# A block of paged key scores cut into two halves, with a prompt pair's scores between them

## What is computed

```python
def block(args):                       # prompt: 16 heads of 64, query blocks of 128
    qb, cb, pb = args
    logits = (jnp.einsum('bqhd,bkhd->bhqk', qb, k).astype(jnp.float32) * FOX_SCALE
              + cb[..., :, None] - cum[:, :, None, :])
    logits = jnp.where(pb[:, None] >= k_pos[None, :], logits, NEG_INF)
    p = jax.nn.softmax(logits, axis=-1).astype(v.dtype)
    return jnp.einsum('bhqk,bkhd->bqhd', p, v)
...
k_past = k_pool[page_table].reshape(b, -1, FOX_HEADS, FOX_DH)      # sample: 16 pages of 128 keys each
v_past = v_pool[page_table].reshape(b, -1, FOX_HEADS, FOX_DH)
logits = (jnp.einsum('bqhd,bkhd->bhqk', q.astype(k_all.dtype), k_all).astype(jnp.float32) * FOX_SCALE
          + suffix[:, :, None, :] - suffix[:, :, p_len:, None])
p = jax.nn.softmax(logits, axis=-1).astype(v_all.dtype)
o = jnp.einsum('bhqk,bkhd->bqhd', p, v_all).reshape(b, n, FOX_HEADS * FOX_DH).astype(x.dtype)
```

## Time and profile before

| | us |
|---|---|
| median of three runs | 3735.44 |
| lowest, highest | 3734.29, 3739.70 |
| the profiled execution | 3732.01 |
| its span in the trace | 3730.4 |
| steady part of the FoX stage in it | 1156 to 1567 |

### The profile page before, as it was taken

The page is one execution under the profiler, slowest core; times in us unless marked ns, Lnnn a source line. Parts: engine busy times, 40 slices in busy tenths (PEclk is TensorE's granted clock), DMA queues, the critical chain, the costliest instruction groups (busy, mean ns, idle before and its releaser), DMA issues.

```text
span 3730.4 us, 65316 instructions
## 1 busy us (share of the span) xinstructions
PE 3241.8 (87%) x27579; PEld 2943.6 (79%) x27579; DVE 1602.6 (43%) x2086; ACT 971.4 (26%) x1423; POOL 244.7 (7%) x331
## 2 busy tenths in 40 slices
PE   7998899997977888869999854479999899889997
PEld 6897799997864444469999743479998798779997
DVE  2324544324224444354442399664432422464422
ACT  2301322223202233232222244332222310232222
POOL 0000000003300000000000078000000000000000
PEclk9996899998987888889999887689999898789998
DMA  3213223322337776632323110123232120322321
GB/s 95 57 34 102 74 86 88 91 74 65 89 105 269 303 297 257 236 94 85 90 86 89 45 45 23 40 63 89 86 89 63 57 79 23 113 68 87 91 86 47
DMA packets 466048, 369.42 MB, mean 99 GB/s; under 512 B 16777, under 2 KB 429886, under 8 KB 465884
## 3 DMA queue, kind: packets, MB, share of 16 engines
q1 hardware_dynamic: 449808, 348.72, 29.6%
q10 hardware_dynamic: 11980, 17.28, 1.4%
q0 software_dynamic: 4096, 1.06, 0.3%
HBM read 348.68 MB, written 17.26 MB: 98 GB/s over the span
## 4 chain that ended last, share of the span: by engine, by line
PE 81%; DVE 9%; issue 5%; ACT 3%; DMA 1%; ACTq 0%; DVEq 0%; SPq 0%
PE acc L716 55%; PE acc L697 6%; PE acc L1049 3%; DVE big L1297 3%; PE acc L1092 2%; PE acc L912 2%; PE acc L900 1%; DVE rstd L1327 1%; PE acc L1010 1%; PE acc L776 1%; PE acc L1001 1%; PE acc L985 1%; DVE yT L1361 1%; PE acc L1225 1%; PE acc L990 1%
## 5 line engine op out<-in xcount | busy, mean ns | idle before, releaser
L716 PE MATMUL acc<-h_hi,wsp 128*128 128x272 f32 x5632 | 944.0, 290 | 66.1 <-DVE h_lo L1583 66.1
L1319 DVE TENSOR_TENSOR wsp<-ring,wsp 128x1024 fp32r<-128x1024 f32 (+1 forms) x320 | 416.8, 1305 | 1169.1 <-ACT wsp L1880 1169.1
L716 PEld LDWEIGHTS acc<-h_hi,wsp 128*128 128x128 f32 x5632 | 798.6, 190 | 68.7 <-issue 68.4
L1880 ACT ACTIVATE wsp<-ring 128x1024 fp32r<-128x1024 f32 (+1 forms) x320 | 358.6, 1124 | 1303.2 <-PE acc L716 1294.1
L716 PE MATMUL acc<-h_lo,wsp 128*128 128x272 f32 x3328 | 690.2, 289 | 0.0
L716 PEld LDWEIGHTS acc<-h_lo,wsp 128*128 128x128 f32 x3328 | 527.2, 190 | 0.0
L716 PE MATMUL acc<-g_hi,wsp 128*128 128x272 f32 x2816 | 473.9, 290 | 24.0 <-DVE g_lo L1578 24.0
L716 PEld LDWEIGHTS acc<-g_hi,wsp 128*128 128x128 f32 x2816 | 401.3, 191 | 24.9 <-issue 24.9
L716 PE MATMUL acc<-i_hi,wsp 128*128 128x272 f32 x1536 | 265.6, 295 | 37.2 <-DVE i_lo L1347 32.4
L716 PE MATMUL acc<-g_lo,wsp 128*128 128x272 f32 x1408 | 292.7, 290 | 0.0
L716 PEld LDWEIGHTS acc<-i_hi,wsp 128*128 128x128 f32 x1536 | 225.0, 196 | 39.7 <-issue 35.6
(11 more groups left out here) (288 smaller groups left out, 3104.6 us busy)
## 6 DMA issues: line engine op xcount, KB each, us to landing
ring<-in_ffn_w SPq DMA_DIRECT2D x176, 512.0 KB, 3.8
mix<-in_cache_fox_k SPq DMA_DIRECT2D x128, 512.0 KB, 6.9
ring<-in_cache_fox_v SPq DMA_DIRECT2D x106, 512.0 KB, 6.9
ring<-in_ffn_w SPq DMA_DIRECT2D x64, 704.0 KB, 4.7
ring<-in_conv_w SPq DMA_DIRECT2D x24, 512.0 KB, 3.9
mix<-in_cache_fox_v SPq DMA_DIRECT2D x22, 512.0 KB, 6.6
ring<-in_gla_wr SPq DMA_DIRECT2D x16, 512.0 KB, 4.0
ring<-in_gla_wv SPq DMA_DIRECT2D x16, 512.0 KB, 4.1
```

Of the source, the lines that this page charges most:

```text
L716: last = pe.matmul(acc[:, bank + h, 0:HALF], wsp[:, s, w, k * P:(k + 1) * P], rhs[:, k0 + k, h * HALF:(h + 1) * HALF], start=start and k = ...
L1319: dve.tensor_tensor(wsp[:, s, 1, 0:tiles * P], ring[:, slot, 0:tiles * P], wsp[:, s, 0, 0:tiles * P], ALU.subtract).then_inc(wlo_done, 1)
L1880: act.activation(wsp[:, slot % SPLITS, 0, 0:tiles * P], ring[:, slot, 0:tiles * P], ACT.Copy)\
```

## The change

sample_scores is cut in two functions. sample_bias has the bias matmuls and the waits; sample_scores(G, heads, new) has the key scores of two of the four head groups, and with new = True the new keys behind them. In an even step the order becomes: bias, first half, turn_output, scores_of_pair, second half with new keys, and only there ksc_full is set. The weighings stand one by one between the item transposes. The transpose of the new probabilities moves from turn() into weigh(v, 0).

On VectorE the pair's maxima come first in an even step, then the reciprocals, then the transposes and the maximum of z; in an odd step transpose 5 stands between the two maxima. On ScalarE the eviction of a block to z moves behind the pair's exponentials, and the exponential of z behind the copies of the pair's transposed probabilities. No instruction's form changes and none is added except a few waits.

```diff
-            def sample_scores(G):
+            def sample_bias(G):
...
                 pe.wait_ge(turned, KG * (G + 1))
-                for c in range(GH4):
+
+            def sample_scores(G, heads, new):
+
+                b, half = G // HALVES, G % HALVES
+                NK = KG * 32
+                for c in heads:
...
-                if half == HALVES - 1:
+                if new and half == HALVES - 1:
...
-                last.then_inc(ksc_full, 1)
+                return last
...
-                    pe.wait_ge(orow_done, b)
-                    pe.transpose(acc[0:NS, 5, 256:256 + P], z[:, KEYS:ZN], ident[:]).then_inc(pn_full, 1)
...
+                    pe.wait_ge(orow_done, b)
+                    pe.transpose(acc[0:NS, 5, 256:256 + P], z[:, KEYS:ZN], ident[:]).then_inc(pn_full, 1)
+                if g == 0:
+                    pe.wait_ge(pt_out, v + 1)
...
-                    if s % 2 == 0 and 2 <= s <= 2 * DB * HALVES:
-                        sample_scores(s // 2 - 1)
+                    scored, G = s % 2 == 0 and 2 <= s <= 2 * DB * HALVES, s // 2 - 1
+                    if scored:
+                        sample_bias(G)
+                        sample_scores(G, (0, 1), False)
                     if 0 < s <= PAIR_STEPS:
                         turn_output(s - 1)
                     if pair:
                         scores_of_pair(s)
+                    if scored:
+                        sample_scores(G, (2, 3), True).then_inc(ksc_full, 1)
                     if v >= 0:
                         weigh(v, 0)
+                    if pair:
+                        turn_item(2 * s)
+                    if v >= 0:
                         weigh(v, 1)
                     if pair:
-                        turn_item(2 * s)
+                        turn_item(2 * s + 1)
...
-                    if more:
-                        turn_pages(G, (3, 4, 5) if s % 2 else (0,))
+                    if more and s % 2:
+                        turn_pages(G, (3, 4))
+                    if pair:
+                        for x in range(2):
+                            n = item(2 * s + x)[2]
+                            dve.wait_ge(sc_full, 2 * s + x + 1)
+                            dve.tensor_reduce(nmax[:, x:x + 1], acc[:, 6 + x, 0:n], AX.X, ALU.max, negate=True)\
+                               .then_inc(pmax_done, 1)
+                            if more and s % 2 and x == 0:
+                                turn_pages(G, (5,))
...
+                    if more and s % 2:
+                        turn_pages(G, (6, 7))
...
+                    if more and s % 2 == 0:
+                        turn_pages(G, (0,))
                     if scored:
...
+                    if more and s % 2 == 0:
+                        turn_pages(G, (1, 2))
```

More of the change, by code:

```diff
@@ L1056, in sample_scores @@
                                 h = GH4 * j + c
-                                last = pe.matmul(acc[32 * j:32 * (j + 1), 1, new], qz[NS:2 * NS, h, f, :],
+                                last = pe.matmul(acc[32 * j:32 * (j + 1), 1, NK:NK + NS], qz[NS:2 * NS, h, f, :],
                                                  k_rep[:, 2 * (c % 2) + f, h // 2, :], start=False,
@@ L1649, in attention @@
                     more = 0 < G < DB * HALVES
-                    if more:
-                        turn_pages(G, (3, 4, 5) if s % 2 else (0,))
+                    if more and s % 2:
[8 more added lines that the diff above has]
+                                turn_pages(G, (5,))
+                    if v > 0 and v % GR == 0:
+                        output(v // GR - 1)
+                    if more and s % 2:
+                        turn_pages(G, (6, 7))
+                    if pair:
+                        for x in range(2):
+                            dve.wait_ge(pexp_done, 2 * s + x + 1)
+                            dve.reciprocal(rsum[:, x:x + 1], rsum[:, x:x + 1]).then_inc(rinv_done, 1)
+                    if more and s % 2 == 0:
+                        turn_pages(G, (0,))
                     if scored:
@@ L1660, in attention @@
                             dve.tensor_reduce(nmx[:, b % 2:b % 2 + 1], mx, AX.X, ALU.max, negate=True).then_inc(nmx_done, 1)
-                    if pair:
-                        for x in range(2):
-                            n = item(2 * s + x)[2]
-                            dve.wait_ge(sc_full, 2 * s + x + 1)
-                            dve.tensor_reduce(nmax[:, x:x + 1], acc[:, 6 + x, 0:n], AX.X, ALU.max, negate=True)\
-                               .then_inc(pmax_done, 1)
-                    if v > 0 and v % GR == 0:
-                        output(v // GR - 1)
-                    if more:
-                        turn_pages(G, (6, 7) if s % 2 else (1, 2))
-                    if pair:
-                        for x in range(2):
-                            dve.wait_ge(pexp_done, 2 * s + x + 1)
-                            dve.reciprocal(rsum[:, x:x + 1], rsum[:, x:x + 1]).then_inc(rinv_done, 1)
+                    if more and s % 2 == 0:
+                        turn_pages(G, (1, 2))
                     if v >= 0 and v % GR == GR - 1:
@@ L2152, in fox @@
                         act.activation(ptb[:, v % 2, :], acc[:, 4, :], ACT.Copy).then_inc(pt_out, 1)
+                    if 0 < s <= PAIR_STEPS:
+                        q, h, n = item(2 * s - 2)
+                        act.wait_ge(ob_full, s)
+                        act.activation(big[:, h // 2, q * P:(q + 1) * P], acc[:, 6, 0:P], ACT.Copy).then_inc(ob_out, 1)
+                    if v >= 0 and v % GR == 0:
+                        act.wait_ge(pn_full, v // GR + 1)
+                        act.activation(p_new, acc[0:NS, 5, 256:256 + P], ACT.Copy).then_inc(pn_out, 1)
+                    if pair:
+                        for x in range(2):
+                            n = item(2 * s + x)[2]
+                            act.wait_ge(pmax_done, 2 * s + x + 1)
+                            act.activation(probs[x][:, 0:n], acc[:, 6 + x, 0:n], ACT.Exp, bias=nmax[:, x:x + 1],
+                                           accum_out=rsum[:, x:x + 1]).then_inc(pexp_done, 1)
                     scored = s % 2 == 0 and 2 <= s <= 2 * DB * HALVES
@@ L2160, in fox @@
                             act.wait_ge(pt_full, GR * (b - 1) + GR // HALVES * (half + 1))
+                            if half == HALVES - 1:
+                                act.wait_ge(pn_full, b)
                         if half == HALVES - 1:
```

33 lines of the change are left out of this document (8 added, 25 removed).

## The result

The changed kernel takes 3682.06 us (median of four runs, 3671.41 to 3684.07) against 3736.18 us: ratio 0.985, 95% interval 0.983 to 0.987, so 54 us are gained. The forecast was 3698, 37 us gained, with a range from 3670 to 3735. The profiled execution took 3680.91 us, with a span of 3679.3, 51.1 us less than before.

The account below looks back on a forecast made before the run. TensorE sets the pace in paged attention, stopping for instruction pages with low clock behind. Terms 21 + 28 + 6 - 13 - 5 = 37 us take 3732.0 to 3695, or 3698 us for the median; range 3670 to 3735.

Parts of the forecast that it names:

- stops: Key-score blocks of paged attention: waits for instruction pages shrink from 38.4 to 17 us, gain 21 us (6 to 30).
- clock: Steady part: 45 us lost to low clock behind 13 blocks, 8 of 13 regained, gain 28 us (5 to 42).
- output copy: Block steps: wait for ScalarE's copy before prompt scores falls from 1.10 to 0.56 us, gain 6 us (4 to 8).
- odd steps: Steps without a block: one weighing fewer as cover, transpose 5 between the maxima; loss 13 us (8 to 20).
- exponential of z: Every second block: turn() waits for z's eviction, maximum and exponential; loss 5 us (0 to 9).
- forecast condition for failure: Forecast wrong if issue waits stay above 30 us, clock stays 0.85, or odd steps lose over 1.5 us each.
- Which halves stop: Halves holding a whole page: first halves of 11, 13 stop 2.5 us; second halves of 1, 2, 3, 5, 10, 14 1.2 us.
- the load time from the DMA share: Instruction page loads: 5.9 us at DMA share 0.92 and 1.03, 3.6 to 3.7 us at 0.56 or 0.02.
- Rival 1: Clock still falls behind blocks in the steady part, giving 8 us instead of 28: 3718 us; chance 0.17.
- Rival 2: Earlier value loads empty the queues before the block, so no stop is left, 71 us gained: 3664 us; chance 0.08.
- rival 3: Stops move into the halves, above 2.5 us in most blocks, and the clock falls behind each: 3749 us; chance 0.11.

## Why the prediction was right, and where its terms were off

| term (us) | predicted | measured | from |
|---|---|---|---|
| stops | +21 (6 to 30) | +26 | issue waits 38.4 to 12.0 |
| clock | +28 (5 to 42) | +30 | TensorE busy 351.9 to 321.8 (317.9 at the same matmuls) |
| output copy | +6 (4 to 8) | +9 | waits for it 24.6 to 15.5 |
| odd steps | -13 (-8 to -20) | -12 | stretches of odd steps, 8 x 0.95 and 7 x 0.6 to 0.9 |
| exponential of z | -5 (0 to -9) | -4 | waits of 3.0 at the start, 0.2, 0.4, and 0.3 more at the end |
| sum | +37 | +49, the spans say +51 | |

The mechanism was right in the main: issue waits fell by two thirds, the granted clock rose to 0.96 (over 0.92 was forecast), and the forecast condition for failure (issue over 30 us) came only where the split was undone. All terms came inside their bounds but the output copy, and all three gains were forecast too small. Off were these steps:

- **Which halves stop.** I took 5.9 us for loads in first halves and 3.6 in second halves, because page loads end before the second half. Blocks 11 and 13, forecast as the longest with 2.5 us each, stopped for 0.92 us (with the wait for the copy in it) and not at all; blocks 3 and 5, forecast with 1.2 us, for 4.05 and 2.46. The step that failed is the load time from the DMA share: under page loads the transfer starts 0.8 to 4.4 us after the page is entered, and the share doesn't show which it will be. The trace of the kernel before had it already. Beside the four loads of the earlier trace rows that fit the rule stand these that break it, two short ones at a share of 1.03 and a long one at 0.73:

```profile
1333.46:1337.35 3.89, 2.77 (x138) 1.93 (x135) 0.00 (x0) 0.16 (x1) 0.00 (x0) 1.00 1.03 416
1421.41:1424.56 3.15, 2.74 (x130) 1.80 (x130) 0.00 (x0) 0.00 (x0) 0.00 (x0) 1.00 1.03 411
...
1362.89:1368.80 5.91, 2.73 (x128) 1.82 (x128) 0.00 (x0) 0.00 (x0) 0.00 (x0) 0.88 0.73 296
```

The total came near because the errors offset each other, and that was luck.

- **The clock.** I let the fall go in 8 of 13 blocks at 0.41 to 0.45 us per us of half clock. It went in nearly all: half clock is (1 - 0.96)/0.5 x 360 = 29 us in place of 123, and 30.1 us for 94 are 0.32 each (0.36 with the 34.0 us at the same matmuls). More falls went, each worth less; that the product came out is luck too. The sum also priced the stops and the clock as two terms, with the output copy at its length alone, and with the page loads cut, falls stood behind the copy's wait as well.
- **The output copy.** I forecast 0.6 us in all steps. In block steps it is 0.37 us, so 9 us in place of 6. (15 x 0.45 is 6.75, which the sum took as 6.)
- **The odd steps** came out near what was worked, 0.95 us in place of 1.2, and at the place named: 0.45 us of it is the wait for the second exponential, behind transpose 5, and 0.32 us a wait for the first that wasn't forecast. That they can't be given back, since VectorE would be late with kT, the prediction had only as "less than 1 us" of cover.
- **The exponential of z** cost 3 us in the first block with it, where I had 1.5, and next to nothing behind it: TensorE's work between covers it.

Rival 1 (the clock falls all the same) failed because in the trace of the changed kernel no fall began in the steady part behind a stop of less than 2.46 us. Rival 2 (no stop left, 3664) is nearer than rival 3 (3749). Rival 3 happened in another form, in the kernel with the old orders: there the stop doesn't move, but a wait of up to 4.6 us for the exponentials takes its place.

## What to carry to other kernels

A long run of tiny matmuls can outrun its own instructions: here 256 of them ran in 2.63 us, and in the stops of the kernel before the next ones took 3.2 to 5.9 us to come. Look for waits that no semaphore explains and count whether they come at equal numbers of instructions, here 256 or a multiple. Put larger matmuls between such runs, but move with them whatever other engines have in their lists, or the softmax behind it becomes the new hole (41.2 us of waits in the kernel with the old orders); here neither of the two alone gained anything (3752 and 3758 us against 3736). Price a hole of a microsecond or more not by its length alone: look at the granted clock behind it. In the run with holes put in, 22 us of idle time came with 32 us more of busy time.

## What the runs showed that I had not expected

- An instruction load isn't slow as a whole under traffic. The 16 KB move in 0.9 to 1.4 us in nearly all stops and TensorE goes on some 1.4 us behind that, with full or cut page loads; what differs is the wait ahead of the transfer, 0.8 to 1.3 us with the queues nearly empty and up to 4.4 us with pages on the way. Loads of 3.9 us at a DMA share of 1.03 and of 6.7 us at 0.73 stand in one trace.
- Holes of nearly one length brought the clock down or not: 1.12 us did for 10 us, 1.23 us didn't, in the same kernel. In other kernels stops of 2.31 and 2.47 us didn't. What decides between them wasn't settled. Nor was why a fall lasts 3.4 us in one kernel and 17 in another.
- With page loads cut to an eighth, the kernel before takes 3669 us in its one run, less than the median of any version with them.
